# First feed-forward started on the unnormalized residual, S5 preparation moved earlier, skip weight folded into the S5 kernel

## The reference, cut to what matters

```python
def first_block(...):
    h = x
    for l in range(DEPTH):
        h = h + hybrid_mixer(rms_norm(h, norm_mix[l]), ...)
        h = h + memory_cross_attention(rms_norm(h, norm_xattn[l]), mem, ...)
    return rms_norm(h, norm_final)

def _swiglu(x, w_in, w_out):
    a, b = jnp.split(x @ w_in, 2, axis=-1)
    return (jax.nn.silu(a) * b) @ w_out

# second_block, layer 0
h = h + 0.5 * _swiglu(_rmsnorm(h, ffn1_norm[0]), ffn1_w_in[0], ffn1_w_out[0])   # feed-forward 0
u = _rmsnorm(h, mix_norm[0])
h = h + _s5_mixer(u, ...)
# in _s5_mixer, after the scan over time has given the states x_re, x_im:
y = einsum('bsgp,ghp->bsgh', x_re, c_re) - einsum('bsgp,ghp->bsgh', x_im, c_im) + d_skip * ug
y = gelu(y);  return y * sigmoid(y @ w_glu)
```

## Time and profile before

| | us |
|---|---|
| median of 3 runs | 1471.44 |
| the profiled execution, whole | 1466.04 |
| its span, first to last instruction | 1464.3 |
| PE (matmul) busy | 1395.4 (95%) |
| DVE busy | 858.9 (59%) |
| ACT busy | 807.0 (55%) |
| POOL busy | 325.9 (22%) |
| share of PE in the chain that ended last | 83% |
| mean granted TensorE clock | 0.984 |

### The profile page before, as it was taken

One profiled execution on the slowest core, in us unless ns is written; L12 is line 12 of the kernel. 1 busy time (PEld: TensorE's weight loads), 2 busy tenths in 40 slices (PEclk: granted clock), 3 DMA queues, 4 the chain that ended last, 5 costly groups with the idle time before them and its releaser, 6 DMA issues.

```text
span 1464.3 us, 22199 instructions
## 1 busy us (share of the span) xinstructions
PE 1395.4 (95%) x7424; PEld 1153.8 (79%) x7424; DVE 858.9 (59%) x1260; ACT 807.0 (55%) x1326; POOL 325.9 (22%) x375
## 2 busy tenths in 40 slices
PE   7998989999879999979899999999999999999998
PEld 6886878887758888767788888888888875788887
DVE  6537665446666655669665555555555679555553
ACT  7766566674655454532664444765444568464442
POOL 2011000011158988967210000010000015000000
PEclk9999999999989999978999999999999999999999
DMA  9532635531556555310786565478665420365661
GB/s 333 177 96 73 216 116 175 153 103 44 174 127 189 180 166 163 108 29 16 230 257 189 184 189 187 149 163 221 186 187 188 142 78 16 115 201 186 187 191 52
DMA packets 170863, 224.75 MB, mean 153 GB/s; under 512 B 14856, under 2 KB 114288, under 8 KB 170784
## 3 DMA queue, kind: packets, MB, share of 16 engines
q1 hardware_dynamic: 168016, 217.27, 46.8%
q0 software_dynamic: 2288, 6.15, 2.6%
q10 hardware_dynamic: 480, 0.29, 0.1%
HBM read 221.16 MB, written 1.44 MB: 152 GB/s over the span
## 4 chain that ended last, share of the span: by engine, by line
PE 83%; DVE 9%; ACT 5%; issue 2%; POOL 1%; DMA 0%; ACTq 0%; DVEq 0%; POOLq 0%
PE psum L1619 15%; PE psum L1607 11%; PE psum L1609 11%; PE psum L1608 11%; PE psum L390 8%; PE psum L392 8%; PE psum L391 7%; PE psum L416 2%; DVE w_lo L338 2%; PE psum L527 2%; PE psum L1646 1%; PE psum L536 1%; ACT w_hi L330 1%; DVE arena L561 1%; PE psum L2802 1%
## 5 line engine op out<-in xcount | busy, mean ns | idle before, releaser
L1806 DVE TENSOR_TENSOR w_lo<-w_raw,w_hi 128x1024 fp32r<-128x1024 f32 x216 | 283.5, 1314 | 286.9 <-ACT w_hi L1740 286.8
L1740 ACT ACTIVATE w_hi<-w_raw 128x1024 fp32r<-128x1024 f32 x216 | 228.8, 1060 | 309.0 <-PE psum L1609 216.8
L338 DVE TENSOR_TENSOR w_lo<-w_raw,w_hi 128x1024 fp32r<-128x1024 f32 (+5 forms) x191 | 225.5, 1207 | 119.5 <-ACT w_hi L330 118.2
L1607 PE MATMUL psum<-w_hi,x_hi 128*128 128x512 f32 x704 | 281.0, 399 | 1.5 <-DVE x_lo L442 0.7
L1609 PE MATMUL psum<-w_hi,x_lo 128*128 128x512 f32 x704 | 275.5, 391 | 0.0
L1608 PE MATMUL psum<-w_lo,x_hi 128*128 128x512 f32 x704 | 275.0, 391 | 0.0
L330 ACT ACTIVATE w_hi<-w_raw 128x1024 fp32r<-128x1024 f32 (+5 forms) x191 | 193.1, 1038 | 103.5 <-PE psum L392 58.5
L390 PE MATMUL psum<-w_hi,x_hi 128*128 128x512 f32 (+6 forms) x608 | 230.2, 379 | 3.9 <-DVE x_lo L2943 2.3
L392 PE MATMUL psum<-w_hi,x_lo 128*128 128x512 f32 (+6 forms) x608 | 225.5, 371 | 0.0
L391 PE MATMUL psum<-w_lo,x_hi 128*128 128x512 f32 (+6 forms) x608 | 225.2, 370 | 0.0
L1609 PEld LDWEIGHTS psum<-w_hi,x_lo 128*128 128x128 f32 x704 | 132.6, 188 | 28.6
(11 more groups left out here) (415 smaller groups left out, 1824.8 us busy)
## 6 DMA issues: line engine op xcount, KB each, us to landing
w_raw<-in_ffn_w_in SPq DMA_DIRECT2D x352, 256.0 KB, 3.2
w_raw<-in_ffn_w_out SPq DMA_DIRECT2D x176, 256.0 KB, 2.9
w_raw<-in_w_in SPq DMA_DIRECT2D x88, 256.0 KB, 3.6
w_raw<-in_w_out SPq DMA_DIRECT2D x32, 256.0 KB, 3.6
w_raw<-in_w_kv SPq DMA_DIRECT2D x24, 256.0 KB, 2.9
w_raw<-in_mem_wk SPq DMA_DIRECT2D x16, 256.0 KB, 5.6
w_raw<-in_mem_wv SPq DMA_DIRECT2D x16, 256.0 KB, 5.0
w_raw<-in_mem_wq SPq DMA_DIRECT2D x16, 256.0 KB, 6.4
```

The source lines that it names most:

```text
L338: nc.vector.tensor_tensor(w_lo[:, s, 0:size(u)], w_raw[:, s, 0:size(u)], w_hi[:, s, 0:size(u)].bitcast(F32), ALU.subtract).then_inc(lo_rea ...
L1607: nc.tensor.matmul(o, xh, whi, start=(kt == 0), stop=False)
L1740: nc.scalar.activation(w_hi[:, s, :], w_raw[:, s, :], ACT.Copy).then_inc(hi_ready, 1)
L1806: nc.vector.tensor_tensor(w_lo[:, s, :], w_raw[:, s, :], w_hi[:, s, :].bitcast(F32), ALU.subtract).then_inc(lo_ready, 1)
```

## The change

1. **Feed-forward 0 lifts the raw residual.** Its channel factor becomes the product of both norm weights (`norm_final` turned into columns by one small transpose and multiplied in), its token factor the product of both reciprocal roots (`ffn0.scale`). The lifts 0 and 1 stand within the last chunk of the projection `wo1` on PE, 2 and 3 behind the first unit of feed-forward 0. `dve_final` now comes after all lifts have read `h`. `wo1.0` takes the other two PSUM banks (`turn["A"] += 2`): those from which `x_lo` of its own input is read.
2. **S5 parameters earlier.** The exponentials and sines (`act_s5_params`, `_2`) go into the mixer of layer 1, the reciprocal to the start of the memory layer, the transposes (`pe_s5_params`) into `wo1.0`; GpSimd's loads wait for the memory attention and no more for the normalized `h`.
3. **Bias rows** leave the middle of GpSimd's S5 work and go behind its last S5 product, at the start of `pool_kv`.
4. **Angles** go into chunks 8 and 9 of feed-forward 0 (two quarters on VectorE) and right behind GpSimd's last `rotate` (two quarters). The clearing goes from (8, 0) to (7, 5), `act_s5_g` of the second half from (8, 0) to (8, 3).
5. **Skip weight folded.** `d_skip` is added on the diagonal of the matrix of the direct term (`dve_s5_skip`, 4 operations of 128x32 for each half); `dve_y`, GpSimd's scaling of the input and the rows in the order of time go away, and gelu reads PSUM.
6. **Units of `glu`**: the fifth and sixth are loaded first, then 0, 2, 1, 3.

The diff, cut to what is spoken of here:

```diff
--- before.py
+++ after.py
...
+    if l == DEPTH - 1:
+        act_s5_params_2(act)
...
+    if l == DEPTH - 1:
+        pe.wait_ge(loads["final"], 32)
+        b = take(pe, "T", "final.gb")
+        nc.tensor.transpose(psum[:, b, 0:KT], nf_rows[0:KT, :], ident[0:KT, 0:KT]).then_inc(*done("lift_pe", "final.gain_turned"))
...
-        for c in range(2):
-            pe_chunk(pe, f"wo{l}.{c}", tiles_first=None if c else f"mem{l}.olo")
+        turn["A"] += 2
+        pe_chunk(pe, f"wo{l}.0", tiles_first=f"mem{l}.olo", after={2: lambda: pe_s5_params(pe)})
+        pe_chunk(pe, f"wo{l}.1", after={2: lambda: pe_ffn_lift(pe, 0, [0]), 4: lambda: pe_ffn_lift(pe, 0, [1])})
...
+        hi_parts(act, chunk_start(f"wo{l}.1") + RING)
+        act_s5_params_3(act)
+        act_lift(act, "ffx0", KT, ffn_gain(0), pairs=[0, 1])
+        return
...
-        lo_parts(dve, chunk_end(f"wo{l}.0"))
-        dve_s5_reciprocal(dve)
-        dve_residual(dve, f"mem{l}", [f"wo{l}.0", f"wo{l}.1"])
+        def lift_first():
+            lo_parts(dve, ffn_first[0] + 2)
+            dve_lift(dve, "ffx0", KT, ffn_gain(0), pairs=[0])
+        lo_parts(dve, chunk_end(f"wo{l}.1") + 1)
+        dve.wait_ge(*when("final.gain"))
+        dve_residual(dve, f"mem{l}", [f"wo{l}.0", f"wo{l}.1"], before={1: lift_first}, convert=False)
...
-    dve_norm(dve, "final", 20)
-    dve.wait_ge(loads["final"], 16)
-    for c in range(2):
-        for t in range(T):
+    dve.wait_ge(*when("ffx0.turned3"))
+    dve.wait_ge(loads["final"], 32)
+    for t in range(T):
+        for c in range(2):
...
+    hi_parts(act, u0 + 4 if f == 0 else u0 + RING)
-        act_norm(act, f"ffn{f}", i, [FFN_AFTER[f] + ".h11"], [FFN_JUNK[f]])
-        act.wait_ge(*when(f"ffn{f}.rstd"))
+        if f == 0:
+            act_squares(act, "ffn0", lambda t: h[:, t, :], i, D, lambda t: f"final.h1{t}", [FFN_JUNK[f]])
+            hi_parts(act, u0 + 5)
+            act_root(act, "ffn0", i, 2)
+            hi_parts(act, u0 + RING)
+            nc.scalar.activation(ssq[:, 118:119], ident[:, 0:1], ACT.Silu).then_inc(*done("norm_act", "ffn0.silu_table"))
+        else:
+            act_norm(act, f"ffn{f}", i, [FFN_AFTER[f] + ".h11"], [FFN_JUNK[f]])
+        act.wait_ge(*when("ffn0.scale" if f == 0 else f"ffn{f}.rstd"))
...
+def dve_ffn(dve, f, first=None, early=None, lifted=0, hooks={}, next_lift=None, next_weights=True, lifted_hook=None):
-    lo_parts(dve, u0 + RING)
+    if lifted_hook:
+        lo_parts(dve, u0 + 4)
+        lifted_hook()
+    if f:
+        lo_parts(dve, u0 + RING)
-        dve_norm(dve, f"ffn{f}", i)
+        dve_mean(dve, f"ffn{f}", i, 2, D, f"ffn{f}.sq1")
+        if f == 0:
+            lo_parts(dve, u0 + 5)
+        dve_rstd(dve, f"ffn{f}", i, 2)
+    if f == 0:
+        lo_parts(dve, u0 + RING)
+        nc.vector.tensor_tensor(rstd[:, i:i + 2], rstd[:, i:i + 2], rstd[:, 20:22], ALU.mult
+                                ).then_inc(*done("norm_dve", "ffn0.scale"))
+        dve.wait_ge(*when("ffn0.scale"))
...
-    if in_tail:
...
-    for b in range(NBUCKET):
-        if edges[b] is None:
-            continue
-        hi = min(x for x in edges[b + 1:] if x is not None)
-        n = hi - edges[b]
-        step(nc.gpsimd.tensor_copy(bias_r[0:NH, SEQ - hi:SEQ - edges[b]],
...
-    s5_angles(pool, nc.gpsimd, "s5_pool", 3)
+    for n in (2, 3):
+        s5_angles(pool, nc.gpsimd, "s5_pool", n)
...
-    if n == 3:
-        eng.wait_ge(*when("s5.turns2"))
...
+        g = g_rows[h2][:, f * P + 3 * 32:(f + 1) * P]
+        nc.vector.scalar_tensor_tensor(g, same, gcol["d_skip"][:, k:k + 1], g, ALU.mult, ALU.add
+                                       ).then_inc(*done("s5_dve", f"s5.Gd{h2}" if f == HJ // 4 - 1 else f"s5.Gd{h2}.{f}"))
-    pe.wait_ge(*when(f"s5.Gr{h2}"))
+    pe.wait_ge(*when(f"s5.Gd{h2}"))
-    dve.wait_ge(*when("s5.Gt1"))
+    dve.wait_ge(*when("s5.G1"))
...
 def act_y(act, k):
-    act.wait_ge(*when(f"s5.pre{k}"))
-    nc.scalar.activation(y_gelu[k].rearrange("p (c s) -> p c s", s=L4), uT[k].rearrange("p s c -> p c s"), ACT.Gelu_apprx_tanh
-                         ).then_inc(*done("s5_act", f"s5.gelu{k}"))
+    act.wait_ge(*when(f"s5.yt{k}"))
+    y = bank(f"s5.ytb{k}")[:, 0:SEQ].rearrange("p (s c) -> p c s", s=L4)
+    nc.scalar.activation(y_gelu[k].rearrange("p (c s) -> p c s", s=L4), y, ACT.Gelu_apprx_tanh
+                         ).then_inc(*done("s5_act", f"s5.gelu{k}", frees=(f"s5.ytb{k}",)))
...
-        if q >= 2:
-            dve_y(dve, q - 2)
-    dve_y(dve, KT - 2)
-    dve_y(dve, KT - 1)
...
-    dve.wait_ge(*when(f"s5.ut{k}"))
-    dve.wait_ge(*when(f"s5.yt{k}"))
-    y = bank(f"s5.ytb{k}")[:, 0:SEQ].rearrange("p (s c) -> p s c", s=L4)
-    nc.vector.scalar_tensor_tensor(uT[k], uT[k], gcol["d_skip"][:, k:k + 1], y, ALU.mult, ALU.add
-                                   ).then_inc(*done("s5_dve", f"s5.pre{k}", frees=(f"s5.ytb{k}",)))
...
+        sp_units(sp, first + 4 + a, first + 5 + a)
+    for u, x in ((0, "s5.direct3"), (2, "s5.p6.1"), (1, "s5.direct7"), (3, "s5.p7.1")):
+top[0] = common
+bias_r = area("bias_r", 512, at=areas["s5_cos"][0])
...
+    pool.wait_ge(*when(f"s5.x{KT - 1}"))
+    step(nc.gpsimd.memset(bias_r[0:NH, :], NEG), "nsa.bias_mask")
+    pool.wait_ge(*when("s5.relT"))
+    for b in range(NBUCKET):
+        if edges[b] is None:
...
-    dve_final(dve)
-    dve_ffn(dve, 0, next_lift=lambda: [dve_turned(dve, f) for f in range(2)], hooks={S5_GT[1]: lambda: dve_s5_zero(dve)}, in_tail=lambda: [s5_angles(dve, nc.vector, "s5_dve", n) for n in range(3)], next_weights=False)
+    dve_norm(dve, "final", 20)
+    dve_ffn(dve, 0, lifted=2, lifted_hook=lambda: dve_final(dve), next_lift=lambda: [dve_turned(dve, f) for f in range(2)],
```

113 lines of the change are left out of this document (61 added, 52 removed).

## The result

| | before | changed |
|---|---|---|
| median of 5 runs each | 1471.44 us (1467.18 to 1473.16) | 1453.39 us (1453.20 to 1460.13) |
| ratio | | 0.9897 (95%: 0.9878 to 0.9915) |
| span of the profiled execution | 1464.3 | 1451.2 |

What follows compares the result with a forecast made beforehand. TensorE, busy 95% of the span, was taken as the bound. Terms 7.2 + 4.1 + 5.1 + 1.2 + 0.5 + 1.0 + 0.7 = 19.8 us, from the median 1471.44, gave 1451.6 us; 8-in-10 range 1447 to 1460.

Steps and rivals of the forecast that it cites:

- Entry: Start of feed-forward 0, `wo1.0` to the sixth unit: sixth unit at 440.4 against 447.58, gain 7.2 us, bounds 5.0 and 12.1.
- price of the clock: Behind TensorE's 3.3 us wait for the fifth unit of feed-forward 0: lowered clock costs another 1.6 us.
- Chunk 8: Chunk 8 of feed-forward 0: the 2.5 us wait and the lowered clock behind it go, gain 4.1 us, bounds 2.5 and 4.3.
- second rival: VectorE becomes the limit in the new places: gain only 13.6 us, time 1457.8 us; chance 0.22.
- My own mark: Feed-forward 0: a second TensorE wait of 2 us or more there would make the prediction wrong.
- mark on the clock: Feed-forward 0: granted clock 1.00 throughout, behind its first 12 us.
- Tail: End of feed-forward 0: without angles ahead of the last split, the second square comes earlier; gain 5.1 us, bounds 4.0 and 5.6.
- (a): Start of the S5 layer: rows in the order of time and part of their copy go, 1.2 us, bounds 0.5 and 1.5.
- (b): First round of the S5 loop: GpSimd no longer scales beside it, gain 0.5 us, bounds 0 and 0.8.
- (c): S5 loop: the eight `dve_y` operations go, gain 1.0 us, bounds 0 and 2.1.
- (d): Behind the S5 loop: TensorE's wait for the start of `glu` shrinks, gain 0.7 us, bounds 0 and 0.8.
- GpSimd: Feed-forward 0 through S5: products start at 433.9, work ends over 30 us earlier, moved bias copies have about 4 us cover.

Runs made afterwards that it cites:

- e9: The changed kernel run again without an edit: 1455.08 us, ratio 0.9898 to the kernel before.
- e4: Changed kernel, but GpSimd's first products of feed-forward 0 wait until the norm's factor (`ffn0.scale`) is formed: 1455.09 us, ratio 0.9898 to the kernel before.
- e3: Changed kernel, but the fifth weight unit of feed-forward 0 is converted ahead of the normalisation of `h`: 1453.19 us, ratio 0.9887 to the kernel before.
- e11: Changed kernel, but the fifth and sixth weight units of feed-forward 0 are converted ahead of the norm's chain: 1454.44 us, ratio 0.9885 to the kernel before.
- e1: Changed kernel, but all four slices of S5 angles are formed on GpSimd, none on VectorE: 1451.94 us, ratio 0.9871 to the kernel before.
- e8: Changed kernel, but VectorE forms its two quarters of the angles behind the last `f_hid` of feed-forward 0: 1451.80 us, ratio 0.9882 to the kernel before.
- e7: Changed kernel, but VectorE's clearing and ScalarE's six copies are back at (8, 0): 1455.56 us, ratio 0.9893 to the kernel before.
- e6: Changed kernel, but the S5 skip is formed apart again and `glu` units load in the old order: 1457.74 us, ratio 0.9920 to the kernel before.
- e10: Changed kernel plus 16 identity matmuls on TensorE in its idle time before the S5 rows: 1454.82 us, ratio 0.9893 to the kernel before.

## Why the prediction was right, and where its steps were not

The time came 1.8 us from the forecast, within the range. By the forecast's own sum against the profile (19.8, or 1446.2 for the profiled execution) 5.2 us are missing at F.

- **Entry, 7.2.** The steps are in the rows: `wo1.0` behind L1525, a wait of 3.08 (3.3), the fifth unit at 435.93 (436.1), the sixth 8.2 earlier. The price of the clock, 1.6, was not paid in this execution, and in e9, where it was, it cost 0.2. Mis-sized is what comes behind: I had `f_hid` by 440 and let the gain stand. It ended at 442.1, because GpSimd's products stretched the norm's chain by some 2.5 us (e4). The turn itself did not wait for it, but the conversions put off behind the chain (on ScalarE and VectorE six in a row) came late: TensorE waited 0.45 for a `w_lo` and 1.14 for ScalarE's copy, and 8.1 us of lead at 442.30 became 6.1 at 447.96. At B 6.2 are left, 0.9 of them from before A: **5.2 measured**. What was missing in the sum is a term for the work queued behind the norm. That TensorE's wait for the fifth unit is what bounds the gain was wrong (e3, e11).
- **Chunk 8, 4.1.** The wait and its clock went, and came back in chunk 9: **0.5 measured**. The step that failed is the cost of the moved angles, which I left out: their VectorE operations in chunks 8 and 9 had no term. The 4.4 us of the first quarter and the slowed `w_lo` behind it use up the lead that the clearing had given. It was the second rival's mechanism, "VectorE becomes the limit in the new places", at a place that it did not name. e1 and e8 give the 4.1 back, e7 shows that the clearing alone brings nothing. My own mark, a second wait of 2 us in feed-forward 0, came true: this step was wrong while the time was right. The mark on the clock failed with it: 0.61 behind the wait at 601.36, where I had 1.00.
- **Tail, 5.1.** The lift behind the last addition came 4.5 earlier than at C; C to D less the rows gives **5.0**.
- **S5.** (a) 1.2: **1.4**, and the same in e6. (b), (c) and (d), 2.2: **1.5**. The first round gave 1.2 (0.5), the start of `glu` 1.7 (0.7), rounds 2 and 5 to 7 together 1.5 (1.0); rounds 3 and 4 lost 2.9, since TensorE, at 0.50 until 663, now was their limit, as VectorE's waits there show (the rows stand below); in e10, with the clock at 1.00 up to 655, both took 5.3. I had the rounds at 5.2 to 5.4 or shorter, and had not seen that the low clock hides a shorter loop.
- **GpSimd.** The last `rotate` ended at 599.6, ahead of the 600 that I gave as its mark, and 28 us earlier than in the kernel before (627.9). The bias copies ended at 708.7, and `h` was waited for until 720.6: cover 11 us, more than the 4. Behind F nothing of it shows. The prediction's case against the change, that GpSimd's products would hold the fifth unit's `w_lo` for 0.7 us, did not come: it took 1.29 us, as it had started first. They held the small products of the norm behind it (e4), which I had at nothing.
- **A reading.** "Some 0.2 us each" would give 2.4 us for 12 matmuls, not 2.7; the 46 instructions in that stretch include short transposes. The matmuls of a unit start 0.23 us apart in the timeline, and 2.7 is right.

VectorE at the ends of rounds 3 and 4 of the S5 loop:

```profile
658.61 1.29 DVE L2447 TENSOR_TENSOR w_raw<-psum,arena 128x512 f32<-128x512 f32 x2 [1.31 <-PE psum L2293]
...
665.40 1.29 DVE L2447 TENSOR_TENSOR w_raw<-psum,arena 128x512 f32<-128x512 f32 x2 [2.03 <-PE psum L2293]
```

That 1451.6 was so near is in good part luck. The profiled execution took 1453.2 as a whole, 7.0 more than the 1446.2 of the forecast. The forecast then added 5.4, since the kernel before had its median so far above its profiled execution (3 to 5 us in the later measurements); the changed kernel's median lies only 0.2 above its own (its five executions have spans of 1451.2, 1458.2, 1451.2, 1452.5, 1451.4 at clocks 0.987, 0.982, 0.986, 0.986, 0.987). No step gave these 5.2 us, and they leave the 1.8. Nor did a step give the 0.9 us that came ahead of A; their cause was not looked for.

## What to carry to other kernels

Work that is moved into an engine's idle time has to be priced in its new place, with what stands behind it; an edit that clears a wait and one that fills the same engine an instant later cancel, and both look right by themselves. Behind a wait that goes, look for the longest chain beside it before counting the gain: here it ended 6 us after the wait (442.1 against 435.9). With differences of 1 to 5 us compare stretches between events, with the clock's part beside them, and not two spans.

## What the runs showed of the hardware

- Whether TensorE's clock falls behind a wait of 2.2 to 3.1 us differs between executions of one program. Behind the fifth unit (waits of 3.0 to 3.1) it fell in eight profiles (e1, e4 to e10; 1.7 us of the table's brackets, in e7 3.4) and not in the first. In stretches that no edit touches its bracket is 0 or 5 us (135 to 150), and 0, 1.7 or 5 (340 to 355). The Trainium skill's page "TensorE: Matmul & The Clock Gate", Part 1, says that the point of change depends on the phase at which the matmuls fall and varies from run to run. These runs agree that it varies; what it depends on they do not show.
- A VectorE product of 128x2 takes 0.16 us alone and up to 1.14 beside GpSimd's products of 128x512 (e4): in proportion a chain of small operations suffers more from a neighbour than a conversion of 128x1024 does (1.25 us each in the changed kernel's four, 1.93 in e4's).
- Of two instructions that met there, the one that had started first kept its length, and the other ended late: VectorE's 128x2 products ended within 0.03 us of GpSimd's, and GpSimd's took 2.0 instead of 1.06 us where a `w_lo` had started 0.03 to 0.17 us ahead of it.
- A float32 matmul of the 128x128 identity took 0.229 us and is recorded as two instructions (30 in 6.86 us, x60), where a transpose of that size is recorded as one and takes 0.13 (eight in 1.03).
